# Order of work, spare products and a regrouped gated stage in a two-layer decoder step

## The reference

```python
u, v = jnp.split(jax.nn.gelu(h @ w_in, approximate=False), 2, axis=-1)
v = layer_norm(v, ln_g, ln_b)
ws = w_s[:, :tc, :tc] * jnp.tril(jnp.ones((tc, tc), w_s.dtype))
mixed = jnp.einsum('gij,bcjgd->bcigd', ws, vg) + b_s[:, :tc].T[None, None, :, :, None]
return (u * mixed.reshape(B, T, GM_WIDTH)) @ w_out, v
```

## Time and profile before

| | us |
|---|---|
| median of 3 runs | 1528.84 |
| lowest, highest | 1527.64, 1532.05 |
| profiled execution | 1530.2 |
| its span | 1528.5 |
| PE busy in the span | 1502.1 (98%) |
| DVE busy | 1218.0 (80%) |
| ACT busy | 986.5 (65%) |

### The profile page before, as it was taken

How to read it: one execution, slowest core, us unless ns; L and a number is a source line. 1 busy time by engine, 2 the same in 40 slices (tenths; PEclk the granted TensorE clock), 3 DMA queues, 4 the chain that set the end, 5 groups by cost and what they waited for, 6 DMA issues and landing times.

```text
span 1528.5 us, 21855 instructions
## 1 busy us (share of the span) xinstructions
PE 1502.1 (98%) x8309; PEld 1282.1 (84%) x8309; DVE 1218.0 (80%) x1122; ACT 986.5 (65%) x937; POOL 164.7 (11%) x162
## 2 busy tenths in 40 slices
PE   7999989999999999999999999999999999999998
PEld 5887769999997987888888888888888888888887
DVE  5479677666454958888889889889888888888987
ACT  3343565444345477777777777777777777777775
POOL 2455000000000024601001001000000000100100
PEclk9999999999999999999999999999999999999999
DMA  6366773524655439999999999999999999999990
GB/s 207 129 237 242 247 275 111 177 99 165 229 186 175 161 111 349 363 392 383 395 393 383 395 393 382 395 393 384 394 393 371 379 395 369 379 395 366 373 370 32
DMA packets 198937, 457.33 MB, mean 299 GB/s; under 512 B 12013, under 2 KB 15119, under 8 KB 198875
## 3 DMA queue, kind: packets, MB, share of 16 engines
q1 hardware_dynamic: 190802, 439.34, 77.7%
q0 software_dynamic: 4336, 13.15, 3.0%
q10 hardware_dynamic: 3736, 3.99, 0.8%
HBM read 444.43 MB, written 12.03 MB: 299 GB/s over the span
## 4 chain that ended last, share of the span: by engine, by line
PE 83%; DVE 3%; ACT 1%; issue 1%; DVEq 0%; ACTq 0%
PE bank L1996 19%; PE bank L2476 13%; PE bank L2478 13%; PE bank L2477 13%; PE bank L2490 7%; PE bank L2492 7%; PE bank L2491 7%; PE bank L2500 2%; PE bank L2267 1%; PE bank L2371 0%; PE bank L2271 0%; DVE ring_r L1410 0%; DVE wql L1786 0%; PE bank L2451 0%; PE bank L2444 0%
## 5 line engine op out<-in xcount | busy, mean ns | idle before, releaser
L1786 DVE TENSOR_TENSOR wql<-ring,wqh 128x2048 fp32r<-128x2048 f32 x335 | 766.8, 2291 | 107.6 <-ACT wqh L974 106.7
L974 ACT ACTIVATE wqh<-ring 128x2048 fp32r<-128x2048 f32 x334 | 641.4, 1921 | 230.2 <-PE bank L2478 147.8
L2476 PE MATMUL bank<-wqh,xgh 128*128 128x512 f32 x892 | 353.6, 396 | 0.2 <-DVE wql L1786 0.2
L2477 PE MATMUL bank<-wql,xgh 128*128 128x512 f32 x896 | 349.1, 390 | 0.0
L2478 PE MATMUL bank<-wqh,xgl 128*128 128x512 f32 x892 | 348.0, 390 | 0.0
L2478 PEld LDWEIGHTS bank<-wqh,xgl 128*128 128x128 f32 x892 | 167.4, 188 | 35.8
L2476 PEld LDWEIGHTS bank<-wqh,xgh 128*128 128x128 f32 x892 | 167.6, 188 | 34.3 <-DVE wql L1786 1.0
L2477 PEld LDWEIGHTS bank<-wql,xgh 128*128 128x128 f32 x896 | 168.5, 188 | 32.8
L974 ACT ACTIVATE wd<-ring 128x1024 fp32r<-128x1024 f32 x90 | 95.0, 1057 | 128.6 <-PE bank L1996 128.5
L2490 PE MATMUL bank<-wqh,heTh 128*128 128x512 f32 x440 | 171.4, 389 | 0.0
L2492 PE MATMUL bank<-wqh,heTl 128*128 128x512 f32 x440 | 171.2, 389 | 0.0
(11 more groups left out here) (438 smaller groups left out, 2058.9 us busy)
## 6 DMA issues: line engine op xcount, KB each, us to landing
ring<-in_moe_w_gate SPq DMA_DIRECT2D x56, 2048.0 KB, 13.7
ring<-in_moe_w_up SPq DMA_DIRECT2D x56, 2048.0 KB, 13.8
ring<-in_moe_w_down SPq DMA_DIRECT2D x56, 2048.0 KB, 13.8
ring<-in_attn_w_in SPq DMA_DIRECT2D x7, 2048.0 KB, 10.4
ring<-in_ffn_w_gate SPq DMA_DIRECT2D x5, 2048.0 KB, 8.6
ring<-in_ffn_w_up SPq DMA_DIRECT2D x5, 2048.0 KB, 7.8
ring<-in_cache_k SPq DMA_DIRECT2D x16, 512.0 KB, 12.9
ring<-in_cache_v SPq DMA_DIRECT2D x16, 512.0 KB, 5.3
```

Of the source, the lines that this page charges most:

```text
L974: return nc.scalar.activation(dst, src, ACT.Copy)
L1786: return v.tensor_tensor(dst, src, head.bitcast(F32), ALU.subtract)
L2476: mm(bank, xgh[:, k, :], w_h[:, part], start=(k == 0), stop=False)
L2477: mm(bank, xgh[:, k, :], w_l[:, part], start=False, stop=False)
```

## The change

- Start: fifteen spare products of `ones` and `ident` are issued before the wait for the parameters. The chunks of x are copied out of PSUM by ScalarE, and VectorE scales them from `xT`. The products of the indexer's weights are put between those of query projections 3 and 4 and of the index key, one by one.
- Ring: the halves of the value weights go to slots 0 and 1, the first key page tile to slot 6 (`early`, `stream_slot`, `held_before`); the wait for the indexer moves with the latter.
- Six spare products in bank `so` before the cached values.
- Output projection: `take_out_weights(m + OW)` goes before `raw_heads(m)`; the last `raw_tail` goes before the feed-forward quarter's tail.
- Gated stage: order gu 0 to 2, sample rows of v as a plain product (`gvs`, as in stage 2), gu 3, v for the two prompt groups of rows and the sum of the strips, turns of `w_s`, gu 4 to 7. VectorE only subtracts the mean and multiplies by the reciprocal deviation; `ln_g` is applied as a scalar per partition when a mixed bank is read, and `ln_b` through eight small products with `wsT`, added to the bias tile. The output rows are multiplied and shifted later, beside the output projection. The statistics are taken by halves.

```diff
+    early = {RING - 1: 0, RING: 1, RING + 1: RING - 1}
+    def stream_slot(n):
+        return early.get(n, n % RING)
+    def held_before(n):
+        return max((k for k in range(n) if stream_slot(k) == stream_slot(n)), default=None)
...
+        for c in range(KD):
+            act.wait_ge(*A.full(("xt", c)))
+            copy(xT[:, c, :], A.ap(("xt", c))[:, 0:T]).then_inc(a_act, 1)
...
         for m in range(KD):
-            raw_heads(1, "wo", [m], hU)
             if 1 <= m and m + OW < KD:
                 take_out_weights(m + OW)
+            raw_heads(1, "wo", [m], hU)
...
+        for c in range(3):
+            drain(c)
+        dve.wait_ge(*A.full(("gvs", 1)))
+        tails_before(GV0 + 2)
+        drain(3)
+        tails_before(GV0 + QU + WD - 1)
+        row_stats(0)
+        tails_before(GU4 + WD)
+        row_stats(1)
...
+        for q in range(2):
+            dve.wait_ge(*A.full(("shift", q)))
+            v.tensor_tensor(bsb[:, 4 * q:4 * q + 4, :], bsb[:, 4 * q:4 * q + 4, :],
+                            A.ap(("shift", q))[:].rearrange("p (g i) -> p g i", g=4), ALU.add).then_inc(a_dve, 1)
...
-            v.tensor_tensor(hL[:, g, 0:NP].rearrange("p (c i) -> p c i", c=2),
-                            bank[:, 0:NP].rearrange("p (c i) -> p c i", c=2),
-                            bsb[:, g, :].unsqueeze(1).broadcast_to([P, 2, P]), ALU.add)
+            v.scalar_tensor_tensor(out=hL[:, g, 0:NP].rearrange("p (c i) -> p c i", c=2),
+                                   in0=bank[:, 0:NP].rearrange("p (c i) -> p c i", c=2), scalar=lnT[:, g:g + 1],
+                                   in1=bsb[:, g, :].unsqueeze(1).broadcast_to([P, 2, P]), op0=ALU.mult, op1=ALU.add)
...
+        for _ in range(15):
+            mm(B.ap(("ssq", 0))[:, 0:P], ones[:], ident[:], start=True, stop=True)
...
+        for p in range(2, 4):
+            A.room(pe, ("qi", p))
             for c in range(KD):
+                index_weight(p - 2, c)
+                last = mm(A.ap(("qi", p))[:, 0:T], w3("qi")[:, c, P * p:P * p + P], hE[:, c, :],
+                          start=(c == 0), stop=(c == KD - 1))
...
+        project_split(("gu", 0), GU0, hL_r, 2 * KD + 1)
+        sum_of_squares(2)
+        for m in range(1, 3):
+            project_split(("gu", m), GU0 + m, hL_r)
+        pe.wait_ge(hs_ok, 2)
+        for half in range(2):
+            A.room(pe, ("gvs", half))
+            weights(("gv", half))
+            for c in range(KD):
+                rows = slice(NS * (c % 4), NS * (c % 4) + NS)
+                last = mm(A.ap(("gvs", half))[rows, :], hs[:, c, :], w3(("gv", half))[:, c, :],
+                          start=(c < 4), stop=(c >= 4), skip_group_check=True)
+            last.then_inc(a_full, 1)
+        project_split(("gu", 3), GU0 + 3, hL_r)
...
+        for q in range(2):
+            A.room(pe, ("shift", q))
+            for j in range(4):
+                g = 4 * q + j
+                last = mm(A.ap(("shift", q))[:, P * j:P * j + P], lnb[:, P * g:P * g + P], wsT[:, g, :], start=True, stop=True)
+            last.then_inc(a_full, 1)
```

More of the change, by code:

```diff
@@ L379, in build @@
     for c in range(KD):
[L380 removed]
+        A.add(("xt", c), "act")
     B.add(("ssq", 0), "act")
@@ L447, in build @@
     B.add(("ssq", 2), "act")
+    for c in range(3):
+        A.add(("gu", c), "dve")
+    for half in range(2):
+        A.add(("gvs", half), "act")
+    A.add(("gu", 3), "dve")
     for half in range(2):
@@ L452, in build @@
         A.add(("wst", q), "act")
-    for c in range(KD):
+    for c in range(4, KD):
         A.add(("gu", c), "dve")
-        if c == 1:
+        if c == 5:
             A.add("wsr", "dve")
+    for q in range(2):
+        A.add(("shift", q), "dve")
     for g in range(8):
@@ L1233, in _, with gelu_of @@
         nc.scalar.activation(rt[:], sums[:, 0:T], ACT.Sqrt, bias=epst[:, 0:1], scale=1.0 / D).then_inc(b_act, 1)
+        heads_before(GV0 + 2)
+        for half in range(2):
+            act.wait_ge(*A.full(("gvs", half)))
+            copy(gv[:, 2, CH * half:CH * half + CH], A.ap(("gvs", half))[:]).then_inc(a_act, 1)
+        def gelu_of(c):
+            act.wait_ge(*A.freed(("gu", c)))
+            nc.scalar.activation(gu[:, c, :], gu[:, c, :], ACT.Gelu).then_inc(gelu_ok, 1)
+        for c in range(4):
+            if c == 3:
+                heads_before(GV0 + WD)
+            gelu_of(c)
         for half in range(2):
@@ L1247, in _ @@
         nc.scalar.activation(mv[0:NS, 2, 2:3], mv[0:NS, 2, 1:2], ACT.Sqrt, bias=epst[0:NS, 0:1]).then_inc(lnroot, 1)
[L1248 to L1253, removed]
+        for c in range(4, KD):
+            heads_before(GU4 + c - 3 + WD)
+            gelu_of(c)
         h_heads(mix_ok, 0)
@@ L1747, in row_norm @@
                 yield
         norming = row_norm()
-        for c in range(KD):
-            dve.wait_ge(*A.full(("gu", c)))
-            v.tensor_tensor(gu[:, c, :], A.ap(("gu", c))[:, 0:T], rt[:], ALU.mult).then_inc(a_dve, 1)
-            tails_before(GU0 + c + 1 + WD)
-            if c == 1:
+        for c in range(4, KD):
+            drain(c)
+            tails_before(GU4 + c - 3 + WD)
+            if c == 5:
                 dve.wait_ge(*A.full("wsr"))
+                v.tensor_copy(lnT[:], A.ap("wsr")[:, 64:72])
@@ L1762, in _ @@
-                last.then_inc(wsS_ok, 1)
-            else:
-                for _ in range(2 if c == 0 else 3):
-                    next(norming, None)
+                v.tensor_tensor(wsS[:].rearrange("p g (b i) -> p g b i", i=TS),
+                                wst4[:].unsqueeze(2).broadcast_to([NS, 8, NSEQ, TS]),
+                                bmask[:].unsqueeze(1).unsqueeze(3).broadcast_to([NS, 8, NSEQ, TS]), ALU.mult)\
+                 .then_inc(wsS_ok, 1)
+            next(norming, None)
```

156 lines of the change are left out of this document (88 added, 68 removed).

## The result

| | before | after |
|---|---|---|
| median of 7 runs each, us | 1529.77 | 1520.79 |
| lowest, highest | 1527.64, 1532.05 | 1517.31, 1523.54 |
| profiled execution, its span | 1530.2, 1528.5 | 1522.76, 1521.1 |

The ratio is 0.9938, with a 95% interval from 0.9927 to 0.995: 9.0 us faster, where 14.8 were forecast. The time lies inside the range (1508 to 1521), by 0.2 us, and outside the forecast's own one (1511 to 1517). The seven executions stand in three groups, and each is listed with the mean granted clock over its span: 1517.3 and 1517.4 at 1.000; 1520.4 and 1520.8 at 0.997; 1522.8, 1523.5 and 1523.5 at 0.995 to 0.996.

A forecast was written before the change was run, and what follows sets the result against it. TensorE was taken to bound the kernel, so time won before the expert loop moves it forward one for one. Terms -8.1 - 0.5 - 2.0 - 4.2 = -14.8 gave 1514.0 us; own range 1511 to 1517, 8 in 10: 1508 to 1521.

The forecast's parts named there:

- Part 1: Start: spare products, faster turns and interleaved index weights bring TensorE to the index keys' turns at 38.0 us: -8.1 us.
- if the clock stays up: Start: at full clock ScalarE's copy paces turns at 0.4 us a chunk, gaining 3.65; two projections then gain 2.25.
- rival A: Start: clock lost in the turns, gain 2.0 there and 0 for two projections instead of 5.9; 1518 us, chance 0.20.
- Its signs: Start: wrong if two first projections take over 9 us; whole forecast wrong if expert loop starts under 10 us earlier.
- the floor: Index keys' turns: they need GpSimd's doubled pages, copied by 35.15 us, so TensorE gains at best -10.9 us.
- Part 2: Value weights loaded early into ring slots 0 and 1: the 0.5 us wait goes, -0.5 us; six spare products count 0.
- Rival D: Before the cached values: value pages come late, TensorE waits one to four us; 1515.5 to 1518.5, up to 1520.5; chance 0.07.
- Part 3: Output projection: heads taken first bring the residual cycle from 4.27 to about 3.1 us; -2.0 us, from -2.6 to 0.
- Part 4: Gated stage: plain sample-row product and less VectorE work start the mixing 4.75 us earlier, mixing itself +0.5; -4.2 us.
- B: Gated stage: VectorE's queue is the bound, so -1 instead of -4.2 us; 1517 us, chance 0.12.
- C: Start: the index weights' loads hide too, down to the page copy's end at 35.15 us; 1511 us, chance 0.08.
- E: Start: clock never rises before the first split projection, +12 less 6.7 of the other parts; 1534 us, chance 0.03.

The follow-up runs named there:

- pages on ScalarE: samples apart, with the copy doubling the index-key pages made by ScalarE behind its four first weight heads instead of by GpSimd: 1516.6 us, ratio 0.9905.
- routing spares: Changed kernel plus 15 ordinary products in the routing stage, in TensorE's waits and between its groups of turns: 1517.8 us, ratio 0.9917.
- gap filled: Changed kernel with 21 instead of 15 spare products ahead of the turns at the start: 1523.7 us, ratio 0.9946.
- all spares: Changed kernel with 21 spare products at the start, 5 at the output projection and 15 in the routing stage: 1517.6 us, ratio 0.9916.
- old index order: all spares, with the index-weight products back behind four query projections and before the index keys: 1517.5 us, ratio 0.9914.
- copy on VectorE: all spares, with both passes over the turned input on VectorE again, as in the kernel before: 1517.5 us, ratio 0.9919.
- samples apart: all spares, with the sample rows' 8 index-weight products together ahead of the index keys instead of between them: 1517.7 us, ratio 0.9919.
- the two other profiles with the old start: Kernel before with only the output heads' reordering (1527.0 us, ratio 0.9978), and with only the gated-stage change (1528.8 us, ratio 0.9988).

## Why the prediction was right or wrong

**Part 1 failed, at the step "if the clock stays up" and by rival A.** The clock fell 1.2 us into the turns. Its signs said so: both projections took 10.64 us (over 9), and the expert loop began 7.4 us earlier, not 10, so that by its own sign the forecast was wrong as a whole. That the median still lies in the range is owed to the range's width and to how many of the seven executions lost the clock, not to the mechanism. The forecast had the spare products end at 8.5 and the turns begin at 9.58, and took that idle microsecond for nothing. The profiled starts put side by side: with a wait of 1.0, 1.3 and 1.7 us between spares and turns the clock fell (pages on ScalarE, the changed kernel, routing spares); with none to 0.6 us it stayed (gap filled, all spares, old index order, copy on VectorE, samples apart); with 1.4 us and ordinary products for turns it stayed too. So in these runs it took both, a wait and transposes. The mere length of the stretch without ordinary products doesn't sort them: where the clock fell, it did so 2.3 to 3.5 us behind the last spare product, and where it stayed, that stretch lasted 4.5 to 5.1 us. The Trainium skill's rule that a transpose is not counted as activity ("TensorE: Matmul & The Clock Gate", Part 4: PE-mode transpose) would let them do it alone; where no wait stood before them the clock outlasted 4.4 us of them. It is not certain in each execution: by the mean clock, two of seven of the changed kernel, and four of five with routing spares, kept the clock with 15 spares. The length of the wait differs from run to run, since the parameters land between 8.5 and 9.5 us.

What part 1 gains with the clock held is 5.5 us at the plain value product (101.49 to 95.98), not 8.1, and 4.5 if the 100.46 and 100.52 of the two other profiles with the old start are the measure. Three of its terms were off; the two projections at full pace took 8.03 us, forecast 7.92. A chunk of turns takes 0.54 us, not 0.4, and the reason given for 0.4 (the copy moves to ScalarE) has no effect: 4.41 us either way. The eight pairs of the index keys take 0.84 us, not 0.62 (2 x 0.2475 and 2 x 0.064): 1.7 us more; the sixteen pairs before them took 0.71, reckoned at 0.74. And the floor: I took the page copy (35.15) for the only one, and wrote that the engines that feed TensorE "move along". VectorE's low halves don't, because GpSimd's tails move by 1.7 us only (35.85 to 34.17): they stood behind ScalarE's first head and now stand behind the page copy, which waits for the pages. The trace of before shows them ending (45.17) 1.1 us before the low halves begin (46.26).

**Part 2**: -0.7, forecast -0.5. No wait, and the 32 records run through (3.64 us instead of 1.92 + 0.52 + 1.92). The six spare products gained and cost nothing: 2.0 us ahead before and behind them. Rival D did not occur. No run has part 2 alone.

**Part 3**: -2.9, beyond the -2.6 I allowed. The mechanism was right (residuals 3.2 us apart). The size was taken from the listed waits (2.2 us); the rest were pauses too short to be listed. Without them the stretch is 4.1 + 7 x 3.17 + 3.2 us of records, 29.5, and that sum, against 32.3, was the bound to use.

**Part 4**: TensorE -3.7 to the mixing and VectorE 61.4 us behind the feed-forward stage, where 61 was forecast against 65.6; the stall of 1.2 is there (4.44 us for the first gate chunk instead of 3.2). Two terms were mis-sized. VectorE begins the mixing 4.2 us earlier, not 4.75. And I charged one of the two three-operand operations of a group: they take 0.48 and 0.24 against 0.42 and 0.18, so eight groups last 10.6 instead of 9.6 us: +1.0, not +0.5. Net -3.2 for -4.2.

**The routing stage** wasn't in the forecast, because nothing in the diff touches it: 0.7 us in the profiled execution, 4.1 in that of the gap-filled kernel (53.9 us from the mixing to the expert loop, 49.8 without a fall), which reached the mixing 2.9 us sooner than the changed one and the expert loop 0.5 later.

The books, by the profile of before: parts 1 to 4 at a full clock are -5.5 - 0.7 - 2.9 - 3.2 = -12.3; the all-spares kernel shows -12.4 (1530.0 to 1517.6), and the changed kernel's own executions at 1.000 lie there too, at 1517.3. The forecast's other 2.5 us are the terms above. The falls of the clock cost the median a further 3.4 us. Rival A priced the fall at 4 us (measured 4.4) and gave 1518, with the other terms as forecast; those 2.5 us bring it to 1520.5, where the middle group and the median lie. That this is the median is in part luck: rival A knew nothing of the routing stage, and how often it falls moved the seven executions between the groups. Its chance of 0.20 was too low for what its own row showed. Rivals B, C, E did not occur: C could not, by the floor.

## What to carry to other kernels

When a saving rests on TensorE's clock, look for every stretch of waits, turns and narrow products behind it, also those that the edit doesn't touch, and put ordinary products on data at hand into the waits there: here that brought the median 3 us and took most of a spread of 6 us away. Before moving TensorE forward by several microseconds, write down for each engine that feeds it what it does in that stretch and what starts it. To see what a change is worth when times fall into groups, list the granted clock of every execution, and compare those at 1.000; a slow start before the first rise isn't in that figure.

## What the hardware showed that I had not expected

The granted clock reads 1.00 before its first rise even while TensorE works at half pace: of the gap-filled kernel's spare products 9 records start between 2 and 4 us and 18 between 6 and 8 us, both under 1.00. The profile's record of the clock begins with the first rise, at 5.2 us there, at 7.5 in the changed kernel and at 20.8 in the kernel before; what lies ahead of it is read as 1.00 for want of a record. The pace of records is the safer reading at a start.

Where the clock fell, it did so for 3.4 to 13.7 us; the changed kernel fell for 3.4 us in one place and 10.2 in another. At the output projection 3.4 us of it cost 1.7 (16 records in 5.81 instead of 4.12).

On ScalarE's queue at the start of the gated stage, the issue behind that of `w_s` took 3.29 us, its five neighbours 0.33 to 1.32, and TensorE had no wait from it. It isn't the shape of the load: in the kernel after it is `ln_g` as 8 rows of 128, in the kernel before `ln_g` on all partitions, at 3.76 us. Why is not shown.
